# One of two hybrid layers, its state-space stage: where dt and D are applied, and in which order weighing is done

## What is computed

```python
xbc = silu(dwconv3(xbc, conv_w, conv_b))          # xs (1024), bm (4x128), cm (4x128)
for d in range(2):                                # forward, backward
    dt    = softplus(dt_raw + dt_bias[d])
    la    = dt * -exp(a_log[d])                   # log decay of 16 heads
    v     = xs * dt                               # per head
    # per chunk, cum = cumsum(la):
    decay = exp(where(lower, cum_i - cum_j, -inf))
    y     = (C_i . B_j) * decay_ij @ v_j  +  (C_i . S) * exp(cum_i)
    S     = S * exp(last) + B^T @ (v * exp(last - cum))
    y    += d_skip[d] * xs
y_ssm = rms_norm((y_fwd + y_bwd) * silu(z)) * norm_gain
```

## Time and profile before

| | |
|---|---|
| runs | 2003.55, 2003.09, 2001.47 us; median 2003.09 |
| the profiled execution's own time | 1998.44 us |
| its span | 1996.6 us, mean granted TensorE clock 0.989 |
| PE busy | 1914.2 us (96%) |
| DVE, ACT, POOL busy | 1273.6 us (64%), 810.1 us (41%), 159.9 us (8%) |
| instructions | 33556 |

### The profile page before, as it was taken

How to read it: one execution, slowest core, us unless ns; L and a number is a source line. 1 busy time by engine, 2 the same in 40 slices (tenths; PEclk the granted TensorE clock), 3 DMA queues, 4 the chain that set the end, 5 groups by cost and what they waited for, 6 DMA issues and landing times.

```text
span 1996.6 us, 33556 instructions
## 1 busy us (share of the span) xinstructions
PE 1914.2 (96%) x13575; PEld 1816.4 (91%) x13575; DVE 1273.6 (64%) x2084; ACT 810.1 (41%) x1349; POOL 159.9 (8%) x130
## 2 busy tenths in 40 slices
PE   7998889999998999999999999989999999999999
PEld 4998779999997989999999989966688999999999
DVE  4565853576776887868978786656536553554553
ACT  4545533222336255324324335555534551441441
POOL 0011620000001000000000024511100000000000
PEclk9998989999999999999999999999999999999999
DMA  8221002344340423443443332100012222222222
GB/s 304 85 77 43 12 12 85 113 141 148 97 147 12 148 85 105 139 131 128 130 146 116 108 107 67 55 12 1 1 43 60 75 76 74 74 67 81 74 68 79
DMA packets 57066, 175.97 MB, mean 88 GB/s; under 512 B 7552, under 2 KB 9472, under 8 KB 56832
## 3 DMA queue, kind: packets, MB, share of 16 engines
q1 hardware_dynamic: 55152, 172.17, 26.9%
q10 hardware_dynamic: 1808, 2.36, 0.3%
HBM read 170.05 MB, written 4.46 MB: 87 GB/s over the span
## 4 chain that ended last, share of the span: by engine, by line
PE 84%; DVE 9%; ACT 3%; issue 2%; DMA 1%; SPq 0%; POOL 0%; ACTq 0%; DVEq 0%
PE ps L379 70%; PE ps L2092 2%; PE ps L2077 2%; DVE t_sb L772 1%; PE ps L1301 1%; DVE h_lo L782 1%; PE ps L879 1%; DVE w_lo L368 1%; DVE PT L2209 1%; PE ps L2045 1%; PE ps L1288 1%; ACT w_hi L360 1%; PE ps L2044 1%; DMA x<-in_x 1%; PE ps L1275 1%
## 5 line engine op out<-in xcount | busy, mean ns | idle before, releaser
L379 PE MATMUL ps<-h_hi,w_hi 128*128 128x320 f32 x2768 | 637.8, 311 | 7.6 <-DVE w_lo L368 2.6
L379 PE MATMUL ps<-h_lo,w_hi 128*128 128x320 f32 x2768 | 633.1, 310 | 9.5 <-DVE h_lo L782 8.4
L379 PE MATMUL ps<-h_hi,w_lo 128*128 128x320 f32 x2768 | 629.7, 308 | 0.0
L368 DVE TENSOR_TENSOR w_lo<-raw,w_hi 128x1024 fp32r<-128x1024 f32 (+1 forms) x218 | 267.0, 1225 | 461.6 <-ACT w_hi L360 461.3
L360 ACT ACTIVATE w_hi<-raw 128x1024 fp32r<-128x1024 f32 (+1 forms) x221 | 230.5, 1043 | 697.7 <-PE ps L379 697.5
L379 PEld LDWEIGHTS ps<-h_lo,w_hi 128*128 128x128 f32 x2768 | 461.2, 188 | 17.0 <-DVE h_lo L782 15.4
L379 PEld LDWEIGHTS ps<-h_hi,w_hi 128*128 128x128 f32 x2768 | 460.3, 188 | 16.7 <-issue 6.6
L379 PEld LDWEIGHTS ps<-h_hi,w_lo 128*128 128x128 f32 x2768 | 462.8, 188 | 0.0
L379 PE MATMUL ps<-hid_hi,w_hi 128*128 128x320 f32 x704 | 161.5, 310 | 4.5 <-DVE hid_lo L981 2.5
L379 PE MATMUL ps<-hid_hi,w_lo 128*128 128x320 f32 x704 | 160.8, 309 | 0.0
L379 PE MATMUL ps<-hid_lo,w_hi 128*128 128x320 f32 x704 | 160.7, 309 | 0.0
(11 more groups left out here) (280 smaller groups left out, 2094.4 us busy)
## 6 DMA issues: line engine op xcount, KB each, us to landing
raw<-in_ffn_up SPq DMA_DIRECT2D x88, 512.0 KB, 3.6
raw<-in_hyb_in SPq DMA_DIRECT2D x49, 512.0 KB, 3.8
mrawB<-in_w_modB SPq DMA_DIRECT2D x48, 512.0 KB, 4.2
mrawA<-in_w_modB SPq DMA_DIRECT2D x64, 256.0 KB, 2.8
raw<-in_ffn_down SPq DMA_DIRECT2D x32, 448.0 KB, 3.3
raw<-in_hyb_out SPq DMA_DIRECT2D x16, 512.0 KB, 3.8
raw<-in_ffn_down SPq DMA_DIRECT2D x16, 512.0 KB, 3.6
modw<-in_w_modA SPq DMA_DIRECT2D x12, 512.0 KB, 12.8
```

What stands on the lines that cost most here:

```text
L368: eng.tensor_tensor(w_lo[:, i % 2, 0:n], raw[:, b % RAW, 0:n], w_hi[:, i % 2, 0:n].bitcast(F32), SUB).then_inc(S("w_lo"), 1)
L379: last = pe.matmul(pj(f)[:, hh, :], w[:, i % 2, k * 128:(k + 1) * 128], v[:, k, hh * HALF:(hh + 1) * HALF], start=(k == 0 and n == 0), sto ...
```

## The change

The exponent takes ln(dt) with it: `ncum` becomes ln(max(dt, 1e-37)) minus the cumulated decay, so that `E` holds decay times dt and the product `xd` is dropped; `pe_out` takes x itself. The two directions of `E` are added before they are multiplied by the scores, so `weigh` is an addition and a multiplication of 640 columns in place of one multiplication of 1280. D times x goes to ScalarE, two activations a pair after its second decay load. GpSimd is left with the two `xw`, in two buffers, from the third pair on gated by silu 16 and by the states two pairs back. The splits of the second `z` unit move behind the stage, and the copy of the second score product ahead of the last silu. In the opening, modulation tiles and rows are put ahead of slices of `dt` and `xs`.

```diff
-        xw = A("xw", [128, 2, NCH, 128])
-        xd = A("xd", [128, 2, 2, NCH, 128])
+        xw = A("xw", [128, 2, 2, NCH, 128])
+        lnd = A("lnd", [128, NCH, 2, SH])
...
         def pe_ssd_in(pe):
-            for k in range(2):
-                pe_slice(pe, dt_, k)
-                pe_mod_unit(pe, 10 + k)
+            pe_slice(pe, dt_, 0)
+            pe_mod_unit(pe, 10)
+            pe_mod_unit(pe, 11)
+            pe_slice(pe, dt_, 1)
+            pe_mod_cols(pe, 2)
+            for m in (12, 13, 14, 15):
+                pe_mod_unit(pe, m)
             pe_slice(pe, dt_, 2)
-            pe_mod_cols(pe, 2)
-            pe_mod_unit(pe, 12)
+            pe_mod_cols(pe, 3)
             pe_slice(pe, dt_, 3)
-            for m in (13, 14, 15):
-                pe_mod_unit(pe, m)
-            pe_slice(pe, xs_, 0)
-            pe_mod_cols(pe, 3)
-            for k in (1, 2, 3):
+            for k in range(4):
                 pe_slice(pe, xs_, k)
...
         def act_cum(act):
+            act.wait_ge(S("dt_max"), 1)
+            act.activation(lnd[:, :, :, :], lnd[:, :, :, :], ACT.Ln).then_inc(S("dt_ln"), 1)
...
                     if name == "bc" and r == 7:
-                        act_split(act, s.u0 + r + 2)
+                        act_G(act, 1)
...
         def dve_cum(dve):
-            dve.tensor_scalar(ncum[:, :, :, :], CUM, -1.0, None, MUL)
+            dve.wait_ge(S("dt_ln"), 1)
+            dve.tensor_tensor(ncum[:, :, :, :], lnd[:, :, :, :], CUM, SUB)
...
-                    low_split(dve, s.u0 + r + 2)
+                    if name == "xs" or r < 7:
+                        low_split(dve, s.u0 + r + 2)
...
                         dve_T(dve, "da", 0, daTM[:, :, :])
+                        dve.wait_ge(S("tp_read"), tp_base["da"] + 1)
+                        dve.tensor_scalar(lnd[:, :, :, :], daTM[:, :, 0:64].rearrange("p c (d h) -> p c d h", d=2)[:, :, :, 0:SH],
+                                          1e-37, None, MAX).then_inc(S("dt_max"), 1)
...
             for c in chunks:
-                for d in range(2):
-                    for r in range(2):
-                        pe.matmul(TP[64 * r:64 * r + 64, c, :], xd[:, p % 2, d, c, 64 * r:64 * r + 64],
-                                  E[2 * (p % 2) + r][:, d, c, :], start=(d == 0), stop=False)
+                for r in range(2):
+                    pe.matmul(TP[64 * r:64 * r + 64, c, :], xs_chunks(p)[:, c, 64 * r:64 * r + 64],
+                              E[2 * (p % 2) + r][:, 0, c, :], start=True, stop=False)
...
+        def act_skip(act, p):
+            for r in range(2):
+                ins = act.activation(Tx[:, p % 2, :, 64 * r:64 * r + 64], xs_chunks(p)[:, :, 64 * r:64 * r + 64], ACT.Copy,
+                                     scale=dsum[:, 2 * p + r:2 * p + r + 1])
+            ins.then_inc(S("ssd_x"), 1)
+
         def act_ssd(act):
+            act.wait_ge(S("tp_read"), tp_base["xs"] + 8)
+            act.wait_ge(S("set"), 6)
             act.wait_ge(S("cum_d"), 2)
-            act_G(act, 1)
...
                         act_decay(act, p, i)
+                        if i == 1:
+                            act_skip(act, p)
...
-                    dve.tensor_tensor(e, e, bcT[:, p // 2:p // 2 + 1, 0:640].to_broadcast([128, 2, 640]), MUL).then_inc(S("ssd_pt"), 1)
+                    dve.tensor_tensor(e[:, 0, :], e[:, 0, :], e[:, 1, :], ADD).then_inc(S("ssd_s"), 1)
+                    dve.wait_ge(S("ssd_s"), 2 * p + r + 1)
+                    dve.tensor_tensor(e[:, 0, :], e[:, 0, :], bcT[:, p // 2, :], MUL).then_inc(S("ssd_pt"), 1)
...
-                if p:
-                    pool.wait_ge(S("ssd_kv"), p)
+                if p >= 2:
+                    pool.wait_ge(S("silu"), 16)
+                    pool.wait_ge(S("ssd_kv"), p - 1)
                 for d in range(2):
-                    scaled(xw[:, d, :, :], wdt[:, :, d, 2 * p:2 * p + 2].unsqueeze(3).to_broadcast([128, NCH, 2, 64]))
-                if p >= 2:
-                    tp_full(pool, tpf_at(yuse(p - 2)))
-                for d in range(2):
-                    at = 32 * d + 2 * p
-                    scaled(xd[:, p % 2, d, :, :], daTM[:, :, at:at + 2].unsqueeze(3).to_broadcast([128, NCH, 2, 64]))
-                scaled(Tx[:, p % 2, :, :],
-                       dsum[:, 2 * p:2 * p + 2].unsqueeze(1).unsqueeze(3).to_broadcast([128, NCH, 2, 64]))
+                    scaled(xw[:, p % 2, d, :, :], wdt[:, :, d, 2 * p:2 * p + 2].unsqueeze(3).to_broadcast([128, NCH, 2, 64]))
...
         def act_z(act):
             s = stages["z"]
+            act_split(act, s.u0 + 1)
...
         def dve_z(dve):
             s = stages["z"]
+            low_split(dve, s.u0 + 1)
...
-            act_apply(act, "norm00", gain(0, 0), gate(0, 0), lambda: act_split(act, MA + 1), None, {2: 2, 3: 3})
+            act_apply(act, "norm00", gain(0, 0), gate(0, 0), lambda: act_split(act, MA + 1), None, {1: 2, 2: 3})
```

More of the change, by code:

```diff
@@ L1268, in pe_states @@
             g = p // 2
-            pe.wait_ge(S("ssd_v"), 5 * p + 2)
+            pe.wait_ge(S("ssd_v"), 2 * p + 2)
             if p:
@@ L1274, in pe_states @@
                 for s, c in enumerate((1, 2, 3, 0) if d == 0 else (4, 3, 2, 0)):
-                    last = pe.matmul(KVP[:, s, d, :], bTM[:, c, g * 128:(g + 1) * 128], xw[:, d, c, :], start=True, stop=True)
+                    last = pe.matmul(KVP[:, s, d, :], bTM[:, c, g * 128:(g + 1) * 128], xw[:, p % 2, d, c, :], start=True, stop=True)
             last.then_inc(S("ssd_kv"), 1)
@@ L1293, in pe_out @@
             if chunks[0] == 0:
-                pe.wait_ge(S("ssd_v"), 5 * p + 4)
                 pe.wait_ge(S("ssd_pt"), 2 * p + 2)
@@ L1392, in dve_ssd @@
                                       ecum[:, 1:5, d, hs].unsqueeze(3).to_broadcast([128, 4, 2, 64]), MUL).then_inc(S("ssd_sc"), 1)
-                dve.wait_ge(S("ssd_v"), 5 * p + 5)
+                dve.wait_ge(S("ssd_x"), p + 1)
                 for d in range(2):
```

## The result

The changed kernel takes 1982.47 us in the median of four runs (1981.53 to 1983.09), where the kernel before takes 2002.28 us in four (1995.18 to 2003.55). The ratio is 0.9909 with a 95% interval of 0.9893 to 0.9925: 15 to 21 us faster. The forecast was 1983.6 us. Run once more beside other kernels, the changed one took 1981.05 us, with a ratio of 0.9905 (0.9881 to 0.9930). One run of the kernel before, among those that stand beside four of the experiments' kernels, took 3088.01 us at a mean granted clock of 0.556 and is left out of the ratios.

A forecast was written before the change was run, and what follows sets the result against it. TensorE, busy 96% of the span, was taken as the bound, so only its waits could yield: 2.0 + 4.4 + 14.6 + 0.9 - 2.4 = 19.5 us. Profiled 1998.44 becomes 1978.9, median 1983.6; range 1979 to 1988.

The forecast's parts named there:

- Opening: Before the last modulation tile TensorE does two slices of 1.08 us less, shortening VectorE's 5.05 us wait; 2.0 us saved.
- End of the input units: Last convolution starts sooner, without GpSimd beside it; first exponentials 4.8 us sooner, 4.4 together with D in pair 0.
- Output and weighing: Pair loop: four matmuls fewer per chunk save 1.1 us a pair; weighing in two operations adds 0.2.
- GpSimd's collision: GpSimd's product enters the gap between addition and multiplication; pairs 3 to 5 take 11.4 us each, 10.0 without collision.
- D on ScalarE: D times x fits ScalarE's idle time from pair 1 on: cost nothing, at the end 1.0 us a pair.
- Tail: From pair 7's inter to the first z matmul, 9.37 us before: 0.9 us less, 2.0 at most.
- Clock: TensorE's 2.3 us stops in pairs 3 to 5 may lower its clock; half of 3 x 1.6 charged, +2.4 us.
- rival D: Slower: TensorE's clock stays at half in the stage because less work leaves it idle too often; 2037 us, chance 0.04.
- A: Smoother: no collision between VectorE's two halves and the clock holds; 26 us less in all, 1977 us, chance 0.14.
- B: Clock falls in each of pairs 1 to 7, costing 11.2 us instead of 2.4; 1992.4 us, chance 0.16.
- C: Opening brings nothing because the last tile comes late; 1985.6 us, or 1987 with a worse pair 0, chance 0.07.
- E: Nothing measurable changes because an unseen wait, such as ScalarE's exponentials, takes over; about 2002 us, chance 0.04.

The follow-up runs named there:

- weigh_whole: Changed kernel with weighing as before, one multiplication of 1280 columns and four matmuls a chunk with x; 1981.78 us, 0.9908 of the kernel before.
- gate_xw: Changed kernel with GpSimd's two `xw` started when inter and `weigh(1)` of two pairs back are done; 1973.93 us, 0.9860 of the kernel before.

## Why the forecast was right, step by step

- **Opening.** Forecast 2.0, measured 2.2. Right, by the step as written; the wait for the third high part was seen but taken to end in time.
- **Logarithm.** No stretch shows it; the projection units after it are as long as before. ScalarE's idle time ahead of the next split went from 3.58 to 1.94 us, the 1.6 that the load and the activation were put at. Costing it at nothing was right.
- **End of the input units.** 4.8 for the first exponential, measured 4.78. Pair 0 then lost 0.74 instead of the 0.4: 0.55 because TensorE went through all of its inter at the lower clock (3.42 us instead of 2.87), and 0.19 ahead of it, where D's two activations now stand in the chain with 0.90 us.
- **Output and weighing.** 1.1 less and 0.2 more a pair: pairs 6 and 7 are at 10.03, where 10.0 stood, and `weigh_whole` is back at 10.9.
- **GpSimd's collision.** Measured in pairs 3 to 5 as worked out, 1.77 and 1.48 us for the two operations, and gone when GpSimd's start was moved. The pairs took 11.2 where 11.4 stood (its own terms, 5.65 + 3.86 + 1.78, give 11.3), and TensorE stopped for 1.97 us instead of 2.3. Without falls of the clock pairs 1 to 7 came to 74.8 against 75.0, with them to 76.1 against 77.4.
- **D on ScalarE.** This is the step that failed, and the total hid it. From pair 1 on it was costed at nothing for ScalarE's idle time. ScalarE had that time, but D's product on GpSimd would hold the next `xw` back, and taking it away lets them slide into the gap: 3.1 us in the pairs (76.1 against 73.0), 1.7 of them by way of the clock. In pair 0, where it was put at 0.4, it costs 0.8: inter starts 5.38 us after the first exponential with it and 4.54 without. The forecast had the collision, though not that this edit was what placed it.
- **Tail.** 0.9 forecast, 0.5 measured; the clock fell earlier in the output and stayed low into z. In `gate_xw`, where it was back before the last copy, it is 0.9.
- **z splits.** Costed at nothing, and rightly: TensorE goes through the first two units without a stop, the moved split being done at 278.1 us while the first unit still runs.
- **Clock.** 2.4 charged, one fall of 1.3 in both profiles. Over the four profiles with these pairs it is six falls in twelve such stops, the half that was charged, at 1.3 us each instead of 1.6 (pair 7 of the kernel before, 13.62 us with a fall and 11.95 without, confirms the 1.6 for its longer output). One sign that was named for being wrong did come, though only just: from the first exponential to the first z matmul the clock was at 0.50 for 15.9 us, where over 15 was named. The kernel before has 21.0 us there by the same count, so the sign was set too low to tell rival D from the forecast.
- **Profile and median.** The profiled execution came out 3.6 us over its own forecast of 1978.9, while the median came out 1.1 under. The late start (3.0), the retention stage (1.2) and the tail with pair 0 (0.8) come to 5.0 against the forecast; the pairs, 13.5 us shorter where 12.2 stood, give 1.3 of it back. The first exponential, forecast 6 to 7 us sooner, came 4.1 sooner in this late start and 7.1 in the second profile. The median of before moved too, from 2003.09 to 2002.28. So that the median fits to 1.1 us is partly luck: the forecast carried over the 4.65 us by which the profiled execution of before lay under its median, and after the change that difference was 0.05.

Of the rivals, A (no collision, no fall) is what `gate_xw` made true on purpose: 1977 stood there, 1973.9 was measured. B, C, D and E did not happen.

The parts of the change are not additive. The kernel with ln(dt) alone in the pairs has nearly all of the gain, and the two edits that look like the main savings on VectorE's and TensorE's side together save only 0.8 us of stretch on top, because the second undoes the first by a shift in time.

## What to carry to other kernels

When two engines hold each other up as VectorE and GpSimd do here, the one off the critical path should be started by an event that fits the other's timetable, not by the earliest moment at which its inputs are ready: two waits were worth 5 us of the stretch here, and without them the matmuls that the change removed brought 1 to 2.5. Splitting an operation in two on the critical engine opens a gap; look up who is waiting for it. And before an engine is relieved of work, ask what that work was holding back.

## What the runs showed of the hardware

The start of the same program, up to the first scaled input, takes 26.1 to 27.5 us or 28.7 to 29.0 us, the latter when TensorE's clock is at 0.50 from 20 to 25 us; the retention stage takes 25.5 to 29.5 us for the same instructions, with a mean granted clock of 0.93 to 0.77. Together these are 7 us, or 0.35% of the kernel, in which two executions can differ though nothing in them was changed. In the pairs of the twelve profiles, no stop of TensorE ahead of the output of 1.6 us or less was followed by the lower clock, those of 1.9 to 2.0 us were in seven of fourteen cases, and those of 3.8 us in all four. GpSimd's product takes 1.25 us undisturbed and 1.38 where it meets a short operation of VectorE in the recurrence; two take 3.5 us where each waits for a 640-column operation.
